# q and k for attention in transfers of 512 KB instead of 256 KB

## The reference, cut to what matters

```
proj = rmsnorm(x) @ w_in            # q, k, v, gates, Fourier input
q, k = rmsnorm(q), rmsnorm(k)       # per head, 12 heads of 64
for window, dil in ((128, 1), (512, 4), (2048, 16)):
    # each query sees itself and 64 keys to either side at steps of dil
    s = q . k / 8 + bias[head, distance];  o_d = softmax(s) @ v;  lse_d = logsumexp(s)
attn = sum over d of softmax(lse)_d * o_d
y = x + concat(attn * silu(gate), fourier(u) * silu(gate2)) @ w_out
```

## Time and profile before

| | |
|---|---|
| median of three runs | 4076.96 us (4073.61 to 4079.73) |
| the profiled execution | 4074.14 us |
| its span, first to last instruction | 4072.4 us |
| mean granted clock of TensorE | 0.964 |
| busy in the span: PE, DVE, ACT, POOL | 92%, 63%, 41%, 10% |
| DMA: moved, mean rate | 721.86 MB, 177 GB/s |
| attention, from its first load to its last instructions | some 2371 to 3462 us of the span |

### The profile page before, as it was taken

One profiled execution on the slowest core, in us unless ns is written; L12 is line 12 of the kernel. 1 busy time (PEld: TensorE's weight loads), 2 busy tenths in 40 slices (PEclk: granted clock), 3 DMA queues, 4 the chain that ended last, 5 costly groups with the idle time before them and its releaser, 6 DMA issues. The chain is left out here.

```text
span 4072.4 us, 100342 instructions
## 1 busy us (share of the span) xinstructions
PE 3766.3 (92%) x38254; PEld 3227.5 (79%) x38254; DVE 2554.1 (63%) x7710; ACT 1680.9 (41%) x4443; POOL 400.9 (10%) x674
## 2 busy tenths in 40 slices
PE   3599999999997999999997859999999999799999
PEld 2488888888886888888884349999989898688887
DVE  3356666666655454445443248888888888777775
ACT  2233333333322111111111148898888888333332
POOL 0000000000000000000000024333342432000000
PEclk7799999999998999999998689999999999899999
DMA  6534444444437554444446996777768675666664
GB/s 131 126 134 154 163 145 140 139 170 142 152 124 234 184 156 141 146 145 144 142 145 168 269 281 169 211 188 188 205 167 214 155 204 137 228 243 244 239 249 175
DMA packets 604151, 721.86 MB, mean 177 GB/s; under 512 B 37215, under 2 KB 473567, under 8 KB 602112
## 3 DMA queue, kind: packets, MB, share of 16 engines
q1 hardware_dynamic: 603840, 717.55, 59.1%
HBM read 383.67 MB, written 337.94 MB: 177 GB/s over the span
## 5 line engine op out<-in xcount | busy, mean ns | idle before, releaser
L474 PE MATMUL p_ps<-p_w_hi,p_h_hi 128*128 128x512 f32 (+1 forms) x3072 | 1144.6, 373 | 22.2 <-DVE p_w_lo L756 20.7
L474 PE MATMUL p_ps<-p_w_lo,p_h_hi 128*128 128x512 f32 (+1 forms) x3072 | 1123.3, 366 | 0.0
L474 PE MATMUL p_ps<-p_w_hi,p_h_lo 128*128 128x512 f32 (+1 forms) x3072 | 1122.6, 365 | 0.0
L1289 ACT ACTIVATE att_p<-att_p,att_o 128x256 f32<-128x256 f32 (+2 forms) x1728 | 682.8, 467 | 125.2 <-DVE att_o L1347 124.2
L474 PEld LDWEIGHTS p_ps<-p_w_hi,p_h_hi 128*128 128x128 f32 x3072 | 582.0, 189 | 116.8 <-issue 18.4
L474 PEld LDWEIGHTS p_ps<-p_w_hi,p_h_lo 128*128 128x128 f32 x3072 | 581.2, 189 | 97.2
L474 PEld LDWEIGHTS p_ps<-p_w_lo,p_h_hi 128*128 128x128 f32 x3072 | 582.2, 190 | 92.1
L1347 DVE CUSTOM_DVE_ANT_0 att_p<-att_ps_s,att_bias 128x256 f32<-128x256 f32 (+2 forms) x1728 | 560.6, 381 | 59.4 <-PE att_ps_s L1227 54.3
L1260 PE MATMUL att_ps_o<-att_v,att_p_low 128*64 128x65 f32 x6528 | 439.7, 225 | 7.7 <-issue 7.4
L1260 PE MATMUL att_ps_o<-att_v,att_p_high 128*64 128x65 f32 x6528 | 439.5, 225 | 7.4 <-issue 7.2
L1260 PEld LDWEIGHTS att_ps_o<-att_v,att_p_low 128*64 128x64 f32 x6528 | 406.3, 140 | 24.6 <-issue 9.6
(11 more groups left out here) (111 smaller groups left out, 5216.4 us busy)
## 6 DMA issues: line engine op xcount, KB each, us to landing
scratch_qk<-p_staging SPq DMA_DIRECT2D x72, 1024.0 KB, 5.8
out_o<-scratch_o SPq DMA_DIRECT2D x144, 396.0 KB, 5.4
att_qk_a<-scratch_qk SPq DMA_DIRECT2D x192, 256.0 KB, 4.5
scratch_o<-att_o SPq DMA_DIRECT2D x168, 264.0 KB, 3.3
p_x<-x SPq DMA_DIRECT2D x48, 512.0 KB, 4.4
scratch_h_t<-p_h_hi SPq DMA_DIRECT2D x48, 512.0 KB, 5.4
scratch_h_t<-p_h_lo SPq DMA_DIRECT2D x48, 512.0 KB, 6.2
p_h_hi<-scratch_h_t SPq DMA_DIRECT2D x48, 512.0 KB, 3.9
```

Of the source, the lines that this page charges most:

```text
L474: ins = pe.matmul(ps[c][:, 0:width[c]], a[s][:, k, :], b[:, k, cols], start=(k == 0 and n == 0), stop=(k == KC - 1 and n == 2))
L1289: ins = act.activation(at, at, ACT.Exp, bias=o[n % BUFS][:, (2 * q + i) % STRETCH, PW + e:PW + e + 1], scale=-1.0)
```

## The change

A piece becomes one part by 1024 tokens: 4096 bytes per partition and 512 KB. Region a has 16 pieces instead of 32, region b 8 instead of 16. A block of 1024 tokens holds four residues of a, so the first block is free for the next pair after round 29. The pieces of a now come one per round in rounds 29 to 35 of the pair before (seven of them) and in rounds 0 to 8 of the pair's own (nine); in pair 0 two per round in rounds 0 to 7, none in round 8. The pieces of b come in every second round from 12 to 26. w_out keeps its rounds. The waits of POOL and PE count 16 times `A_PIECES` or `B_PIECES` as before, thus again all pieces.

```diff
-A_PIECES, B_PIECES = 32, 16
+A_PIECES, B_PIECES, COLS = 16, 8, 2 * BANK
...
                 lanes, part = i // 4, i % 4
-                at = slice(lanes * BANK, (lanes + 1) * BANK)
+                at = slice(lanes * COLS, (lanes + 1) * COLS)
...
-                    if g < 8:
-                        each_round = 4 if opening else 2
-                        for i in range(g * each_round, (g + 1) * each_round):
-                            load_piece_of("a", it, i + A_PIECES - 8 * each_round)
+                    if g < 9:
+                        for i in range(2 * g, min(2 * g + 2, A_PIECES)) if opening else (g + 7,):
+                            load_piece_of("a", it, i)
                     if g == 0 and not opening:
                         load_bias(2, it)
-                    if 12 <= g < 12 + B_PIECES:
+                    if 12 <= g < 12 + 2 * B_PIECES and g % 2 == 0:
                         if more:
-                            load_piece_of("b", it + 1, g - 12)
-                        elif g % 2 == 0:
+                            load_piece_of("b", it + 1, (g - 12) // 2)
+                        else:
                             load_w_out((g - 12) // 2)
                     if g in (20, 28) and more:
                         load_bias(0 if g == 20 else 1, it + 1)
-                    if g >= 28 and more:
-                        for i in range(2):
-                            load_piece_of("a", it + 1, 2 * (g - 28) + i)
+                    if g >= 29 and more:
+                        load_piece_of("a", it + 1, g - 29)
```

## The result

The changed kernel took 4105.4 us in the median of four runs, the kernel before 4078.4 on the same chip: a ratio of 1.0070, 95% interval 1.0052 to 1.0087. A second set of runs beside the experiments gave 1.0067 (1.0054 to 1.0080). It is slower by 27 us, in the direction that was forecast and nearly twice as much as the 14.5 us forecast, outside the range.

What follows compares the result with a forecast made beforehand. The prediction took attention as bound by TensorE, with region a already late in each pair. Its terms, 13 + 4 - 2.5 = +14.5 us, on the median of 4077.0, gave 4091.5 us; range for 8 in 10, 4077 to 4102.

Steps and rivals of the forecast that it cites:

- the last piece of a moves from round 7 to round 8: Attention, pairs 1 to 5: later last piece lengthens TensorE's wait at scores by 2.6 us each, +13 us (6 to 20).
- The issue's part: Pairs 1 to 5: the last piece of a ends its issue later in SP's queue, mean 2.4 us per pair.
- The clock's: After the five longer waits TensorE works longer at the lower clock: 1.1 us a pair, +4 us (0 to 8.5).
- the term of the landing: Pairs 1 to 5: region a complete 2.6 us later, the issue's 2.4 and a little for the queue: +13 us.
- So 0.43 MB of these 1.07 MB had gone: Pair 2's queue: of two rounds issued after a's last piece, this had moved, leaving 0.11 MB of round 8's.
- so the issue decides: Pair 2, round 8: queued bytes ahead plus the piece take 2.4 us, less than the issue's 2.8 us.
- If none of round 8 had gone, it would be 1.06 MB, 4.0 us: Pair 2, round 8: delay of the last piece if all of that round's bytes still stood in front of it.
- the lower bound: Last piece of a lands in the median 4.5 us instead of 5.7, making the delay about 1.2 us.
- the rival that rested on it: Larger transfer lands sooner and pays for the round: delay 1.2 us per pair, 4080.5 us; chance 0.2.
- the rival on the faster side: Queue bound by count of transfers, not bytes: no wait grows, TensorE's other idle time shrinks 5.4 us, 4065.6 us; chance 0.06.
- Gains, -2.5 us: Rows of 4096 bytes and fewer issues shorten the start's wait and pair 0's: -2.5 us (0 to -6).
- strictly in order and the clock falls twice: Rival: queue strictly in order, 4.0 us later in each of five pairs, 8.5 us of clock: +27.5, 4104.5 us; chance 0.09.

Runs made afterwards that it cites:

- small_round8: Kernel before with its 256 KB pieces of a moved to the changed kernel's rounds, 29 to 35 and 0 to 8: 4097.6 us, 1.0058 of the kernel before.
- big_round7: Changed kernel with the last 512 KB piece of a back in round 7, two pieces in round 29: 4080.0 us, 1.0012 of the kernel before.
- big_first: Changed kernel with round 8's piece of a issued ahead of that round's store and values: 4093.1 us, 1.0048 of the kernel before.
- merged_rows2k: Kernel before with each round's two pieces of a as one transfer of two parts, rows still 2048 bytes: 0.9996 of the kernel before.
- big_early: Changed kernel with a's last piece in round 5, 1 MB in rounds 29, 31, 33: 4070.7 us, 0.9988 of before; run again, 4079.0 us, 0.9999.
- small_early_same: Kernel before's 256 KB pieces of a, same bytes per round as big_early (1 MB in rounds 29, 31, 33): 0.9989 of the kernel before.
- merged_early: Kernel before with a in 512 KB transfers of two parts, rows of 2048 bytes, in big_early's rounds: 1.0001 of the kernel before.
- light_after: Changed kernel, each piece of a from pair 1 on loading only its first eighth of tokens: 4069.4 us, 0.9993 of the kernel before.
- light_before: Kernel before, each piece of a from pair 1 on loading only its first eighth of tokens: 4047.3 us, 0.9943 of the kernel before.
- small_early: Kernel before, a's last pieces in round 5, three and two pieces by turns in rounds 28 to 35: 4056.0 us, 0.9948; again 4055.6 us, 0.9966.

## Why the prediction was off by half

**Right: the place and the direction.** The step "the last piece of a moves from round 7 to round 8" is the loss: small_round8 shows it alone at 23 us, big_round7 without it at 5. The waits grew in the five pairs named, pair 0 kept its own, and nothing gave the time back.

**Right: the issue and the clock behind the waits.** The issue's part, 2.4 us per pair, measured 2.6 and 2.4. The clock's, 4 us for five longer waits, measured 4.2 and 4.3.

**Wrong: the term of the landing, 13 us (5 x 2.6).** The step that failed is the one behind the issue: "So 0.43 MB of these 1.07 MB had gone" and "so the issue decides", which left 0.2 us per pair for the queue. It counted what the 16 DMA engines had moved together when region a was complete, and let the new piece stand behind the 0.11 MB left over. But the landing did not stay at 5.7 us after its issue, it took 7.2: 1.5 us more per pair (2.3 in the second profiles) instead of 0.2. GpSimd waits for a's last packet (in ten landings before and ten after it starts 0.5 to 1.3 us behind its end), and bytes that other packets have moved meanwhile do not bring it nearer. The 4.1 us by which GpSimd started later (4.7) are those of the bound "If none of round 8 had gone, it would be 1.06 MB, 4.0 us", and big_first, with 0.54 MB fewer in front, had the landing back at 5.7. TensorE's waits grew by 3.7 us a pair (4.6), 18.3 us (22.9) instead of 13. The larger transfer landing at 4.5 us after its issue, the lower bound and the rival that rested on it, never appeared: the median landing rose from 4.5 to 5.5 us, with twice the bytes in each. The fixed cost per transfer of the Trainium skill ("DMA: Bandwidth & Descriptors", "Anatomy of one DMA") finds nothing here to save: merged_rows2k, half as many transfers of a in the same rounds, is at 0.9996, so the fixed costs of two pieces issued 0.55 us apart do not add up. (Taken as an estimate, its 2.0 us saved would have left 0.4 us of the issue's 2.4, not the 1.2 of the rival that names it.)

**Missing: low clock elsewhere, some 3 to 4 us.** TensorE's busy time grew by 7.2 and 8.2 us, not by the 4.2 and 4.3 behind the five waits. The rest lies mostly in low stretches in attention away from them, such as one of 3.4 us after the idle time of 1.9 us that ends at 2700.1. The prediction had no such term.

**Missing: idle time with nothing behind it, +7 to +10 us.** This is the largest term that it put at nothing. It had 27 us of such time in its own rows but used them only in the rival on the faster side, as something that might shrink. It grew, and it also ate the gain of most of the earlier schedules. What in the change makes it grow is open.

**Gains, -2.5 us.** The start's wait fell by 1.2 and 1.0 us, as put, although the rate of 355 GB/s behind it was read from a stage in which only 137 of some 313 transfers, about half of the bytes, are of 512 KB. Pair 0 gained nothing that repeats (5.0 and 3.3 us against 5.0 and 5.3).

The rival "strictly in order and the clock falls twice", +27.5 us and given 0.09, came out in its time, 4104.5 against 4105.4, and for the landing in its mechanism: 5 x 4.0. That its time fits so closely is partly luck: its 8.5 us of clock are twice what the waits cost, and it has no idle time with nothing behind it.

**What stays open.** The size of the pieces itself: the changed kernel and small_round8, and big_early_again and small_early_same, have the same rounds, big_round7 and before nearly so; each pairing puts the large pieces 0.09% to 0.12% higher, some 4 us, and none does so clearly beyond its interval. The transfers of 512 KB with short rows do not decide it: merged_early is 0.12% above small_early_same, merged_rows2k 0.04% below before. And the idle time with nothing behind it, and how far it differs from execution to execution. It is 9 us larger in light_after than in light_before, but mostly not where a is cut: 3.8 us of it lie in pair 0, where a comes in full, and 3.3 us in the four ninths of pairs 1 to 4 in which b is loaded, in pieces of 512 KB in one kernel and of 256 KB in the other. So b's pieces may have a part in it; no run changes them alone. The two profiles of one kernel differ by 0.7 to 4.7 us, and merged_rows2k's, 44.0 us, is of an execution 12 us above that kernel's own median, so a single profile says little.

## What to carry to other kernels

Before pieces are merged, find the last one that someone waits for and ask in which round it will now be issued: coarser pieces come free later, and here one round cost 23 us where the larger transfers gave back one at the start. When a transfer moves back in a queue that is full, price it with all the bytes issued ahead of it since the old place, not with what the engines have left on average; the landing is that of its last packet. Where a wait stands at such a landing, more pieces per round as early as the buffer allows remove it (small_early: 0.3% to 0.5% faster than before), but evenly: three rounds of 1 MB, or 768 KB in each of eight rounds, gave back all or about half of it.

## What was not expected of the hardware

TensorE's idle time in attention that ends with "issue" depends on the DMA load. The records of packets show 16 KB packets on the instruction queue (q8) some 5.5 us apart in attention, where the code of all six pairs is written out. Every idle time of more than 0.9 us of this kind (8 before, 14 in the changed kernel, 19 in big_early) ends 1.2 to 1.6 us after such a packet has come in; by chance that would be so for about one in fourteen. The packets themselves take no longer (mean 1.08 us before, 1.09 after). So TensorE seems to wait for its own instructions there, and longer where more data fill the same engines: 21 us in all in light_before with 37 MB less of a (5 pairs x 8.4 MB x 7/8), 34 before, 47 to 52 with rounds of 1 MB. That these packets are TensorE's, and that they queue behind data, is inferred from this, not seen in a record.
